# The first projections of a one-core attention and mixture-of-experts step: raw tokens transposed, the norm factor put in at the copies, the first weight block in four pieces, zero products while TensorE waits

## Chip, cores and metric

One core of one Trainium2 chip runs the whole step. The metric is the device time of one execution in microseconds (us). A change of less than 0.2% cannot be told from none by a measurement of this kernel.

## What is computed

The reference is one layer over 256 prompt tokens and 8 × 4 new tokens of a sampled batch, all in float32:

```python
def rmsnorm(x, g):
    xf = x.astype(jnp.float32)
    y = xf * lax.rsqrt(jnp.mean(xf * xf, axis=-1, keepdims=True) + RMS_EPS)
    return (y * g.astype(jnp.float32)).astype(x.dtype)

def project_inputs(x, norm_g, w_in, pos):
    h = rmsnorm(x, norm_g)
    qa, ka, va, qb, kb, vb, qc, gate_logits = jnp.split(h @ w_in, np.cumsum(IN_SPLITS)[:-1].tolist(), axis=-1)
    ...
```

Behind it come three attentions (a window of 128, three dilations, 256 memory tokens, for the sampled batch over caches of 2048 positions), sigmoid gates from `gate_logits` on the merged branches, `w_out`, a second norm, and a mixture of 32 experts of which each token takes 4, with a last norm. The factor 1/sqrt(mean square) is one number for each token (a row of x) and the gain `g` one for each column, so `h @ w_in` is also that factor times `((x * g) @ w_in)`.

## The kernel before

The program is written by hand for each engine, and semaphores hold the engines together; nothing plans the order. The 288 tokens are three tiles t of 128, 128 and 32 (`NTOK`). The model width of 1024 is 8 chunks k of 128.

The start goes like this. SyncE issues the loads in the order of its code: the two prompt tiles (L446, L447), the sampled tokens (L448), the identity matrix (L449), `params` with the gains (L450), weight block 0 (L460), the rest of the constants (L535), weight block 1 (L460). ScalarE takes the sum of squares of each tile as it lands (L699) and its root (L707). VectorE makes the factor of the norm from it (`inverse_roots`, L1657 to L1661). Then the rows of x are multiplied by their factor into `h_tok`: tiles 0 and 2 by VectorE (`scale_rows`, L1665), tile 1 by ScalarE (L718). TensorE transposes h in six groups of four chunks (`transposes`, L1001, against the identity matrix), and VectorE copies each group from PSUM (`ps`) to `hT`, which lies in `arena`, and multiplies it by the gain (`evict_tr`, L1678). Only then come the projections:

```python
for n in range(5):
    wblk_ready(pe, n)
    pe.wait_ge(S["tr_evicted"], 6)
    for t in range(3):
        for k in range(KC): ...
```

There are five blocks n of columns (four of 512, one of 256). A block is two tiles of 8 products of 128x512 (L1034) and the 32 sampled tokens, whose 8 chunks go to four row groups of PSUM and are added by VectorE (L1707 to L1710). The weights have two buffers (`wblk`, in `ring`), and block n + 2 is issued by SyncE when the products of block n are done (`wait_wblk_used`), with a copy of a piece of a cache in HBM behind it (L483). ScalarE copies the projections to `q_tok` and `kv` (L735 to L747), with the fixed factor `QSCALE` for the queries.

In the third block the transposes of the memory tokens (their own norm; L718, L1001) are put in. After the fifth block TensorE waits for the weights of the memory projection (L1043), and after these it transposes the queries and keys (L1001) between the products of the gates (L1065), which read `hT` again, all 288 tokens as the moving operand. VectorE turns the queries and keys before that (`rope`, L1727 to L1732). GpSimd loads the memory tokens when block 0 has landed (L651).

Much later, SyncE starts a stream of 192 pieces of 2 MB of expert weights through eight buffers (L578): each piece is issued when TensorE has used what lay in its buffer before.

## Time and profile before

| what | value |
|---|---|
| three runs | 1329.03, 1330.87 and 1331.73 us, median 1330.87 us |
| the profiled execution | 1324.62 us, its span 1322.8 us |
| TensorE busy in the span | 1275.8 us, 96% |
| VectorE, ScalarE, GpSimd busy | 340.8, 213.0 and 27.5 us |
| mean granted TensorE clock | 0.992 |
| moved by DMA | 498.76 MB |

### The profile page before, as it was taken

What the parts mean: (1) busy time and instruction counts of PE and PEld (TensorE: products, weight loads), DVE (VectorE), ACT (ScalarE), POOL (GpSimd) and SP (SyncE); (2) the same over time, 40 slices, a digit from 0 to 9 for tenths busy, and PEclk for the clock granted to TensorE, in tenths of its full rate; (3) what the DMA queues carried; (4) which work ended last, traced back from release to release, by engine and by line L of the source; (5) the groups of instructions that cost most, each with busy time, mean ns of one, the idle gap of its engine ahead of it and who ended that gap; (6) DMA issues with size and microseconds to landing.
All of it is one profiled execution on the core that took longest, in us unless ns stands there. A gap on an engine that the chain in (4) does not pass through costs nothing.

```text
span 1322.8 us, 14782 instructions
## 1 busy us (share of the span) xinstructions
PE 1275.8 (96%) x6332; PEld 526.7 (40%) x6332; DVE 340.8 (26%) x735; ACT 213.0 (16%) x442; POOL 27.5 (2%) x42
## 2 busy tenths in 40 slices
PE   6999997999999999999999999999999999999996
PEld 3446666667543333333333333333333333333332
DVE  2243552323533221211222122121211212121213
ACT  2212433223111011011110101111011101101012
POOL 0000004200000000000000000000000000000000
PEclk9999998999999999999999999999999999999998
DMA  6675998789779999999999999999999999999994
GB/s 252 253 270 231 355 367 276 227 265 352 294 279 397 402 427 427 428 428 428 427 427 428 427 427 429 429 428 427 429 427 427 428 428 427 428 428 427 428 426 173
DMA packets 71013, 498.76 MB, mean 377 GB/s; under 512 B 5808, under 2 KB 28976, under 8 KB 45584
## 3 DMA queue, kind: packets, MB, share of 16 engines
q1 hardware_dynamic: 70032, 495.15, 92.1%
q0 software_dynamic: 912, 2.62, 0.5%
q8 instruction: 52, 0.85, 0.3%
q14 instruction: 17, 0.14, 0.0%
HBM read 495.29 MB, written 36.96 MB: 402 GB/s over the span
## 4 chain that ended last, share of the span: by engine, by line
PE 81%; DMA 14%; DVE 2%; ACT 1%; issue 0%; SPq 0%; DVEq 0%
PE ps L1540 27%; PE ps L1577 15%; DMA ring<-in_w_gate_up 13%; PE ps L1065 7%; PE ps L1464 6%; PE ps L1509 5%; PE ps L1034 5%; PE ps L1354 2%; PE ps L1346 2%; PE ps L1228 2%; PE ps L1212 1%; PE ps L1475 1%; PE ps L1557 1%; PE ps L1043 1%; PE ps L1517 1%; PE ps L1294 1%
## 5 line engine op out<-in xcount | busy, mean ns | idle before, releaser
L1540 PE MATMUL ps<-ring,cring 128*64 128x512 f32 x1552 | 352.9, 598 | 5.8 <-DMA ring<-in_w_gate_up 5.8
L1540 PEld LDWEIGHTS ps<-ring,cring 128*64 128x64 f32 x1552 | 106.0, 137 | 226.0 <-issue 204.4
L1577 PE MATMUL ps<-ring,cring 128*64 128x512 f32 x752 | 171.5, 598 | 0.7 <-issue 0.7
L1930 DVE TENSOR_TENSOR cring<-ps,params 128x512 f32<-128x512 f32 x32 | 22.1, 691 | 424.2 <-PE ps L1475 424.2
L2028 DVE TENSOR_TENSOR x_tok<-x_tok,ps 128x1024 f32<-128x1024 f32 (+1 forms) x51 | 53.0, 1040 | 225.3 <-PE ps L1509 225.3
L1065 PE MATMUL ps<-arena,ring 128*128 128x288 f32 x384 | 102.3, 412 | 2.1 <-ACT ring L771 2.1
L926 ACT ACTIVATE cring<-ps 128x512 f32<-128x512 f32 x32 | 19.1, 597 | 488.6 <-PE ps L1557 488.6
L1464 PE MATMUL ps<-h_tok,cring 128*64 128x512 f32 x372 | 91.1, 607 | 0.0
L1577 PEld LDWEIGHTS ps<-ring,cring 128*64 128x64 f32 x752 | 50.1, 136 | 102.4 <-issue 99.7
L1065 PEld LDWEIGHTS ps<-arena,ring 128*128 128x128 f32 x384 | 69.6, 189 | 25.6 <-issue 4.6
L1034 PE MATMUL ps<-ring,arena 128*128 128x512 f32 (+3 forms) x240 | 73.1, 561 | 0.5 <-DVE arena L1678 0.5
L1540 PE MATMUL ps<-late,cring 128*64 128x512 f32 x256 | 59.5, 596 | 1.6 <-DMA late<-in_w_gate_up 0.8
L1540 PE MATMUL ps<-arena,cring 128*64 128x512 f32 x240 | 55.8, 595 | 0.0
L936 ACT ACTIVATE cring<-ps 64x512 f32<-64x512 f32 x32 | 18.9, 590 | 226.1 <-PE ps L1577 226.1
L1509 PE MATMUL ps<-cring 128*128 128x512 f32 (+1 forms) x96 | 52.6, 630 | 0.7 <-issue 0.7
L1509 PE MATMUL ps<-pT,cring 128*128 128x512 f32 (+1 forms) x96 | 49.3, 596 | 0.0
L1034 PEld LDWEIGHTS ps<-ring,arena 128*128 128x128 f32 (+1 forms) x240 | 32.7, 165 | 39.8 <-issue 38.9
L1943 DVE TENSOR_TENSOR cring<-cring 128x512 f32<-128x512 f32 x32 | 22.2, 693 | 85.7 <-ACT cring L922 85.6
L1464 PEld LDWEIGHTS ps<-h_tok,cring 128*64 128x64 f32 x372 | 21.1, 134 | 47.1 <-issue 43.4
L1354 PE MATMUL ps<-ring,arena 128*128 128x512 f32 (+1 forms) x96 | 33.4, 599 | 0.0
L918 ACT ACTIVATE cring<-ps 128x512 f32<-128x512 f32 x32 | 19.1, 597 | 86.0 <-PE ps L1464 82.5
L1577 PE MATMUL ps<-arena,cring 128*64 128x512 f32 x144 | 32.8, 597 | 0.0
(325 smaller groups left out, 1001.8 us busy)
## 6 DMA issues: line engine op xcount, KB each, us to landing
ring<-in_w_gate_up SPq DMA_DIRECT2D x97, 2048.0 KB, 24.7
ring<-in_w_down SPq DMA_DIRECT2D x47, 2048.0 KB, 27.1
late<-in_w_gate_up SPq DMA_DIRECT2D x16, 2048.0 KB, 24.3
arena<-in_w_gate_up SPq DMA_DIRECT2D x15, 2048.0 KB, 26.3
ring<-in_w_in SPq DMA_DIRECT2D x10, 2048.0 KB, 11.0
late<-in_w_down SPq DMA_DIRECT2D x8, 2048.0 KB, 26.4
arena<-in_w_down SPq DMA_DIRECT2D x8, 2048.0 KB, 25.8
out_dil_k_s<-in_cache_dil_k SPq DMA_DIRECT2D x8, 2044.0 KB
```

Of the source, the lines that this page charges most:

```text
L1034: ins = pe.matmul(bank((n % 2) * 3 + t)[k_rows(t, k), 0:b - a], hT_v[:, k, TOK0[t]:TOK0[t] + NTOK[t]], wblk[n % 2][:, k, 0:b - a], **k_gro ...
L1065: ins = pe.matmul(bank(gate_bank(m))[:, 0:TT], wblk[(6 + m // 4) % 2][:, k, (m % 4) * P:(m % 4 + 1) * P], hT_v[:, k, :], start=(k == 0), s ...
L1228: return pe.matmul(out, lhs, rhs, start=start, stop=last, skip_group_check=True)
L1346: ins = pe.matmul(bank(3 * (dt % 2) + br)[:, 0:TT], wblk[blk % 2][:, k, (dt % 4) * P:(dt % 4 + 1) * P], oT[:, k, :], start=(k == ks[0]), s ...
L1354: ins = pe.matmul(bank(wout_bank[t][n])[k_rows(t, k), :], hT_v[:, k, TOK0[t]:TOK0[t] + NTOK[t]], wo[n][:, k, :], **k_group(t, k))
L1464: ins = pe.matmul(bank(6)[64 * h:64 * h + 64, :], sel[0:n, t, :], h_v[0:n, t, h * 512:(h + 1) * 512], start=(t == 0), stop=(t == 2), skip_ ...
L1509: ins = pe.matmul(out, gateT[:, tok] if first else selT[:, tok], b_dn[:, 512 * h:512 * h + 512] if first else y2[h], start=True, stop=True ...
L1540: ins = pe.matmul(bank(gu0 + u)[64 * h:64 * h + 64, :], xTe[:, k % 4, (k // 4) * 64:(k // 4) * 64 + 64], pair_buf[slot][:, a:a + 512], sta ...
L1577: ins = pe.matmul(bank(7 if last else 5)[64 * h:64 * h + 64, :], aT[:, kk % 4, (kk // 4) * 64:(kk // 4) * 64 + 64], pair_buf[slot][:, a:a ...
L1930: v.tensor_tensor(xTe4, xps, gain_x, ALU.mult).then_inc(S["xt_ready"], 1)
L1943: v.tensor_tensor(act, u_clip, g_sig, ALU.mult).then_inc(S["act_ready"], 1)
L2028: v.tensor_tensor(xs, xs, rows, ALU.add).then_inc(S["sc_added"], 1)
```

## The change

- The six first transposes take `x_tok` and not `h_tok`, so they wait for the load of x alone. `hT` then holds x times the gain, and the factor of the norm is put in where ScalarE copies the projections (`q_scale`, which is the factor times `QSCALE`, and `norm_st[16..18]`). VectorE makes all three factors at once, after the six copies, and `scale_rows` of VectorE and the ScalarE one for tile 1 are gone.
- The gates read `hT` too. So, after block 4, TensorE multiplies a matrix of ones with a diagonal of the factors (three small products into bank 6), and VectorE multiplies the whole `hT` by the result (128x2304, one instruction between its turns of tile 0 and tile 1). The first transposes of the queries wait for it.
- Weight block 0 is loaded in four pieces of two chunks, and the loads of x tile 1 and of the sampled tokens are issued between them. TensorE's code for block 0 is written out by hand: two products of tile 0 as each piece lands, a group of transposes between them.
- VectorE clears 384 columns of `pT` first, and TensorE multiplies zeros (`warm_up`, 256 columns each, into bank 5, which nobody reads): four before the first transposes, three behind the second group.

```diff
@@ -285,6 +285,9 @@
         norm_st = stat[:, 180:204]
+        q_scale = norm_st[:, 21:24]
+        rstd_diag = pT[:, 0:TT]
+        warm = pT[:, 512:896]
         s_st = stat[:, 204:256]
@@ -294,7 +297,7 @@
             for c in (0, 4):
-                tr_groups.append(([h_v[0:NTOK[t], t, (c + j) * P:(c + j + 1) * P] for j in range(4)],
+                tr_groups.append(([x_v[0:NTOK[t], t, (c + j) * P:(c + j + 1) * P] for j in range(4)],
                                   hT_v[:, c:c + 4, TOK0[t]:TOK0[t] + NTOK[t]], gain_v[:, 0, c:c + 4]))
@@ -444,8 +447,6 @@
             sp.dma_start(x_v[:, 0, :], d["x_prompt"][0, 0:P, :]).then_inc(S["x0_in"], 16)
-            sp.dma_start(x_v[:, 1, :], d["x_prompt"][0, P:SEQ, :]).then_inc(S["x1_in"], 16)
-            sp.dma_start(x_v[0:NS, 2, :], d["x_sample"].rearrange("b i n -> (b i) n")).then_inc(S["x2_in"], 16)
             sp.dma_start(ident, d["consts"][:, 0:P]).then_inc(S["id_in"], 16)
@@ -531,7 +532,16 @@
                 assert 16 * outs == KV_OUT
-            load_wblk(0)
+            def load_first(k, s):
+                a, b = qkv_cols[0]
+                sp.dma_start(wblk[0][:, k:k + 2, :], w_in[:, k:k + 2, a:b]).then_inc(S[s], 16)
+
+            load_first(0, "w0a_in")
+            sp.dma_start(x_v[:, 1, :], d["x_prompt"][0, P:SEQ, :]).then_inc(S["x1_in"], 16)
+            load_first(2, "w0b_in")
+            sp.dma_start(x_v[0:NS, 2, :], d["x_sample"].rearrange("b i n -> (b i) n")).then_inc(S["x2_in"], 16)
+            load_first(4, "w0c_in")
+            load_first(6, "wblk0_in")
             sp.dma_start(cst[:, P:], d["consts"][:, P:]).then_inc(S["cst_in"], 16)
@@ -718,8 +728,6 @@
             act_e.wait_ge(S["rstd"], 1)
-            scale_rows(x_v[:, 1, :], h_v[:, 1, :], P, 1)
-
             for n in range(5):
@@ -730,21 +738,22 @@
                     q, kvt = q_tok[0:r, t, :], kv[0:r, t, :]
+                    qs, ks = q_scale[0:r, t:t + 1], norm_st[0:r, 16 + t:17 + t]
                     if n == 0:
...
                         ins = act_e.activation(q[:, 0:512].rearrange("p (j v n) -> p v j n", v=2, n=HD),
-                                               pb.rearrange("p (v j n) -> p v j n", v=2, n=HD), ACT.Copy, scale=QSCALE)
+                                               pb.rearrange("p (v j n) -> p v j n", v=2, n=HD), ACT.Copy, scale=qs)
                     elif n == 1:
-                        act_e.activation(kvt[:, 0:128], pb[:, 0:128], ACT.Copy)
-                        act_e.activation(kvt[:, 384:512], pb[:, 128:256], ACT.Copy)
-                        ins = act_e.activation(q[:, 512:768], pb[:, 256:512], ACT.Copy, scale=QSCALE)
+                        act_e.activation(kvt[:, 0:128], pb[:, 0:128], ACT.Copy, scale=ks)
+                        act_e.activation(kvt[:, 384:512], pb[:, 128:256], ACT.Copy, scale=ks)
+                        ins = act_e.activation(q[:, 512:768], pb[:, 256:512], ACT.Copy, scale=qs)
                     elif n == 2:
-                        ins = act_e.activation(q[:, 768:1280], pb, ACT.Copy, scale=QSCALE)
+                        ins = act_e.activation(q[:, 768:1280], pb, ACT.Copy, scale=qs)
                     elif n == 3:
-                        act_e.activation(kvt[:, 128:384], pb[:, 0:256], ACT.Copy)
-                        ins = act_e.activation(kvt[:, 512:768], pb[:, 256:512], ACT.Copy)
+                        act_e.activation(kvt[:, 128:384], pb[:, 0:256], ACT.Copy, scale=ks)
+                        ins = act_e.activation(kvt[:, 512:768], pb[:, 256:512], ACT.Copy, scale=ks)
                     else:
-                        ins = act_e.activation(q[:, 1280:1536], pb[:, 0:256], ACT.Copy, scale=QSCALE)
+                        ins = act_e.activation(q[:, 1280:1536], pb[:, 0:256], ACT.Copy, scale=qs)
                     ins.then_inc(S["proj_evicted"], 1)
@@ -1011,32 +1020,68 @@
+            def proj_products(n, t, ks):
+                a, b = qkv_cols[n]
+                for k in ks:
+                    ins = pe.matmul(bank((n % 2) * 3 + t)[k_rows(t, k), 0:b - a],
+                                    hT_v[:, k, TOK0[t]:TOK0[t] + NTOK[t]], wblk[n % 2][:, k, 0:b - a],
+                                    **k_group(t, k))
+                if ks[-1] == KC - 1:
+                    ins.then_inc(S["proj_done"], 1)
+
+            def warm_up(n):
+                for _ in range(n):
+                    pe.matmul(bank(5)[:, 0:256], warm[:, 0:P], warm[:, P:3 * P], start=True, stop=True)
+
+            pe.wait_ge(S["warm_ready"], 1)
+            warm_up(4)
             pe.wait_ge(S["id_in"], 16)
-            for g in range(6):
-                pe.wait_ge(*((S["hn_v"], 1), (S["hn_done"], 1), (S["hn_v"], 2))[g // 2])
-                if g >= 2:
-                    pe.wait_ge(S["tr_evicted"], g - 1)
-                transposes(g)
-
-            for n in range(5):
+            pe.wait_ge(S["x0_in"], 16)
+            transposes(0)
+            transposes(1)
+            warm_up(3)
+            pe.wait_ge(S["tr_evicted"], 1)
+            pe.wait_ge(S["w0a_in"], 16)
+            proj_products(0, 0, range(0, 2))
+            pe.wait_ge(S["x1_in"], 16)
+            transposes(2)
+            pe.wait_ge(S["w0b_in"], 16)
+            proj_products(0, 0, range(2, 4))
+            pe.wait_ge(S["tr_evicted"], 2)
+            transposes(3)
+            pe.wait_ge(S["w0c_in"], 16)
+            proj_products(0, 0, range(4, 6))
+            pe.wait_ge(S["x2_in"], 16)
+            pe.wait_ge(S["tr_evicted"], 3)
+            transposes(4)
+            wblk_ready(pe, 0)
+            proj_products(0, 0, range(6, 8))
+            pe.wait_ge(S["tr_evicted"], 4)
+            transposes(5)
+            proj_products(0, 1, range(KC))
+            pe.wait_ge(S["tr_evicted"], 6)
+            proj_products(0, 2, range(KC))
+
+            for n in range(1, 5):
                 wblk_ready(pe, n)
-                pe.wait_ge(S["tr_evicted"], 6)
-                a, b = qkv_cols[n]
                 for t in range(3):
...
                         for g in range(6, TR_H):
-                            pe.wait_ge(S["hn_done"], g // 2 - 1)
+                            pe.wait_ge(S["hn_done"], g // 2 - 2)
                             pe.wait_ge(S["tr_evicted"], g - 1)
...
                         pe.wait_ge(S["proj_evicted"], 3 * (n - 2) + t + 1)
-                    for k in range(KC):
-                        ins = pe.matmul(bank((n % 2) * 3 + t)[k_rows(t, k), 0:b - a],
-                                        hT_v[:, k, TOK0[t]:TOK0[t] + NTOK[t]], wblk[n % 2][:, k, 0:b - a],
-                                        **k_group(t, k))
-                    ins.then_inc(S["proj_done"], 1)
+                    proj_products(n, t, range(KC))
+            pe.wait_ge(S["cst_in"], 16)
+            pe.wait_ge(S["diag_ready"], 1)
+            pe.wait_ge(S["tr_evicted"], TR_H)
+            for t in range(3):
+                tok = slice(TOK0[t], TOK0[t] + NTOK[t])
+                ins = pe.matmul(bank(6)[:, tok], const("ones")[0:NTOK[t], :], rstd_diag[0:NTOK[t], tok],
+                                start=True, stop=True)
+            ins.then_inc(S["rstd_rows"], 1)
             wblk_ready(pe, W_MEM)
-            pe.wait_ge(S["tr_evicted"], TR_H)
             for t in range(2):
@@ -1078,6 +1123,7 @@
             wblk_ready(pe, 6)
+            pe.wait_ge(S["hT_scaled"], 1)
             pe.wait_ge(S["proj_evicted"], 15)
@@ -1660,11 +1706,7 @@
-            def scale_rows(t):
-                r = NTOK[t]
-                v.tensor_scalar(h_v[0:r, t, :], x_v[0:r, t, :], norm_st[0:r, 16 + t:17 + t], None, ALU.mult) \
-                    .then_inc(S["hn_v"], 1)
-
+            v.memset(warm, 0.0).then_inc(S["warm_ready"], 1)
             link(v.memset(norm_st, 1.0))
@@ -1678,16 +1720,16 @@
-            link(inverse_roots(0, 1, 1))
-            scale_rows(0)
-            signal(inverse_roots(1, 2, 2), "rstd")
             v.wait_ge(S["params_in"], 16)
-            evict_tr(0, 0)
-            evict_tr(1, 1)
-            link(inverse_roots(2, 3, 3))
-            scale_rows(2)
-            for g in range(2, 6):
+            for g in range(6):
                 evict_tr(g, g)
+            link(inverse_roots(0, 3, 3))
+            v.tensor_scalar(q_scale, norm_st[:, 16:19], QSCALE, None, ALU.mult).then_inc(S["rstd"], 1)
+            for t in range(3):
+                r = NTOK[t]
+                ins = v.tensor_scalar(rstd_diag[0:r, TOK0[t]:TOK0[t] + r], ident[0:r, 0:r], norm_st[0:r, 16 + t:17 + t], None,
+                                      ALU.mult)
+            ins.then_inc(S["diag_ready"], 1)
@@ -1714,6 +1756,10 @@
             for t in range(3):
+                if t == 1:
+                    v.wait_ge(S["rstd_rows"], 1)
+                    v.tensor_tensor(hT_v, hT_v, bank(6)[:, 0:TT].unsqueeze(1).to_broadcast([P, KC, TT]), ALU.mult) \
+                        .then_inc(S["hT_scaled"], 1)
                 v.wait_ge(S["proj_evicted"], 12 + t + 1)
```

TensorE's queue from the start of the program, in the kernel before (`x_tok` and `h_tok` are x and its scaled form, `arena` here the identity matrix or `hT`, `ring` the weight block, and [waits ...] names the semaphores that a row waits for):

```order
L1001 MATMUL ps<-arena,h_tok 128x128 [waits hn_v,id_in]
L1001 MATMUL ps<-arena,h_tok 128x128 x3
L1001 MATMUL ps<-arena,h_tok 128x128 [waits hn_v]
L1001 MATMUL ps<-arena,h_tok 128x128 x3
L1001 MATMUL ps<-arena,h_tok 128x128 [waits tr_evicted,hn_done]
```

TensorE's queue at the same place in the changed kernel, to the end of block 0's first tile:

```order
L1034 MATMUL ps<-pT 128x256 [waits warm_ready]
L1010 MATMUL ps<-arena,x_tok 128x128 [waits x0_in,id_in]
L1034 MATMUL ps<-pT 128x256 x3
L1026 MATMUL ps<-ring,arena 128x512 [waits w0a_in,tr_evicted]
L1010 MATMUL ps<-arena,x_tok 128x128 [waits x1_in]
L1026 MATMUL ps<-ring,arena 128x512 [waits w0b_in]
L1010 MATMUL ps<-arena,x_tok 128x128 [waits tr_evicted]
L1026 MATMUL ps<-ring,arena 128x512 [waits w0c_in]
L1010 MATMUL ps<-arena,x_tok 128x32 [waits tr_evicted,x2_in]
L1026 MATMUL ps<-ring,arena 128x512 [waits wblk0_in]
L1010 MATMUL ps<-arena,x_tok 128x32 [waits tr_evicted]
```

Each row with a wait stands for the first of its group; the rest of a group follows without one. The waits for the norm (`hn_v`, `hn_done`) are gone, and six products of tile 0 stand ahead of the last two groups of transposes.

SyncE's queue, in the kernel before:

```order
L446 DMA x_tok<-in_x_prompt 128x1024
L447 DMA x_tok<-in_x_prompt 128x1024
L448 DMA x_tok<-in_x_sample 32x1024
L449 DMA arena<-in_consts 128x128
L450 DMA params<-in_params 128x330
L460 DMA ring<-in_w_in 128x8x512
L535 DMA arena<-in_consts 128x3253
L460 DMA ring<-in_w_in 128x8x512
```

And in the changed kernel:

```order
L449 DMA x_tok<-in_x_prompt 128x1024
L450 DMA arena<-in_consts 128x128
L451 DMA params<-in_params 128x330
L537 DMA ring<-in_w_in 128x2x512
L540 DMA x_tok<-in_x_prompt 128x1024
L537 DMA ring<-in_w_in 128x2x512
L542 DMA x_tok<-in_x_sample 32x1024
L537 DMA ring<-in_w_in 128x2x512 x2
L545 DMA arena<-in_consts 128x3253
L461 DMA ring<-in_w_in 128x8x512
```

The identity matrix moved up to second place; the bytes ahead of the end of block 0, and ahead of the end of block 1, are the same. There are three issues more.

## Rows read from the trace of the kernel before

**Rows 1.** The page: the chain that ended last, shares of the span.

```profile
PE 81%; DMA 14%; DVE 2%; ACT 1%; issue 0%; SPq 0%; DVEq 0%
```

**Rows 2.** Timeline 0 to 15 us: start, duration, instruction [idle before <-releaser].

```profile
0.80 0.08 DVE L1668 MEMSET stat<- 128x24 f32 x1 [0.80 <-PEq L2141]
...
8.00 1.94 PE L1001 MATMUL ps<-arena,h_tok 128*128 128x128 f32 x8 [8.00 <-DVE h_tok L1665]
...
13.04 0.41 PE L1001 MATMUL ps<-arena,h_tok 32*128 32x32 f32 x4 [0.84 <-DVE arena L1678]
...
14.51 31.02 PE L1034 MATMUL ps<-ring,arena 128*128 128x512 f32 x79 [0.48 <-DVE arena L1678]
```

**Rows 3.** Timeline of block 0: two weight loads at half clock; tiles 0, 1; block 1.

```profile
17.34 0.33 PEld L1034 LDWEIGHTS ps<-ring,arena 128*128 128x128 f32 x1 [0.52 <-issue]
18.19 0.33 PEld L1034 LDWEIGHTS ps<-ring,arena 128*128 128x128 f32 x1 [0.52 <-issue]
...
23.35 0.60 ACT L735 ACTIVATE cring<-ps 128x512 f32<-128x512 f32 x1 [12.95 <-PE ps L1034]
...
30.22 0.60 ACT L735 ACTIVATE cring<-ps 128x512 f32<-128x512 f32 x1 [6.27 <-PE ps L1034]
...
31.96 0.30 PEld L1034 LDWEIGHTS ps<-ring,arena 128*128 128x128 f32 x2 [0.84 <-issue]
```

**Rows 4.** Busy time by stretch: PE, PEld, DVE, ACT, POOL, PEclk, DMA share, GB/s.

```profile
13.00:14.00 1.00, 0.77 (x8) 0.64 (x8) 0.77 (x2) 0.00 (x0) 0.67 (x1) 1.00 1.08 455
...
14.50:15.25 0.75, 0.74 (x2) 0.47 (x3) 0.00 (x0) 0.00 (x0) 0.00 (x0) 1.00 0.78 330
15.25:18.65 3.40, 3.40 (x5) 1.33 (x4) 0.96 (x1) 0.00 (x0) 0.00 (x0) 0.50 0.99 384
18.65:20.00 1.35, 1.35 (x4) 0.57 (x3) 0.00 (x0) 0.00 (x0) 0.00 (x0) 1.00 1.05 408
```

**Rows 5.** DMA issues of 0 to 26 us: KB each, median us to landing.

```profile
arena<-in_consts SPq DMA_DIRECT2D x1, 64.0 KB, 5.2
params<-in_params SPq DMA_DIRECT2D x1, 165.0 KB, 5.0
```

**Rows 6.** Landings: both weight blocks of L460, then the three loads of x.

```profile
DMA to landing us min/median/max: 9.9/15.3/20.7
...
DMA to landing us min/median/max: 3.8/5.3/5.4
```

**Rows 7.** Timeline: SyncE's issues of x tile 0, params, weight blocks 0 and 1.

```profile
0.72 0.41 SPq L446 DMA_DIRECT2D x_tok<-in_x_prompt  x1
...
2.59 0.49 SPq L450 DMA_DIRECT2D params<-in_params  x1
3.12 0.43 SPq L460 DMA_DIRECT2D ring<-in_w_in  x1
...
4.22 0.44 SPq L460 DMA_DIRECT2D ring<-in_w_in  x1
```

**Rows 8.** Timeline 60 to 106 us: transposes at full clock, VectorE's turns, the memory block.

```profile
61.59 1.04 PE L1001 MATMUL ps<-arena,ring 128*128 128x128 f32 x8
...
91.82 14.00 PE L1043 MATMUL ps<-ring 128*128 128x512 f32 x32 [1.71 <-DMA ring<-in_w_mem_kv]
...
94.41 0.20 DVE L1732 TENSOR_TENSOR late<-late 128x48 f32<-128x48 f32 x1
...
99.62 0.19 DVE L1732 TENSOR_TENSOR late<-late 32x48 f32<-32x48 f32 x1
...
105.66 1.04 PE L1001 MATMUL ps<-arena,cring 128*128 128x128 f32 x8
```

**Rows 9.** The page's groups: VectorE with a PSUM operand, 128x1024.

```profile
L2028 DVE TENSOR_TENSOR x_tok<-x_tok,ps 128x1024 f32<-128x1024 f32 (+1 forms) x51 | 53.0, 1040 | 225.3 <-PE ps L1509 225.3
```

**Rows 10.** Waits: who <- whom: us in total, times, longest; SyncE's queue first.

```profile
SPq L578 <- PE ps L1540: 507.4, 124, 10.6
...
PE ps L1540 <- DMA ring<-in_w_gate_up: 5.8, 6, 1.2
```

More of the change, by code:

```diff
@@ L226, in build @@
         names = """x0_in x1_in x2_in mem_in id_in cst_in params_in tail_self wblk0_in wblk1_in kc0_in kc1_in
-        out_dma copy_dma v_self zeros sumsq root rstd ssum_ready hn_v hn_done tr_done tr_evicted proj_done
-        proj_evicted rope_done gate_done gate_evicted gates_ready
+        out_dma copy_dma v_self zeros sumsq root rstd ssum_ready hn_done tr_done tr_evicted proj_done
+        proj_evicted w0a_in w0b_in w0c_in diag_ready rstd_rows hT_scaled warm_ready rope_done gate_done gate_evicted gates_ready
         scores_done stat_ready exp_done p_ready pt_done pt_evicted pv_done o_evicted
@@ L1438, in _ @@
             pe.wait_ge(S["sel0_ready"], 1)
-            pe.wait_ge(S["hn_done"], 4)
+            pe.wait_ge(S["hn_done"], 3)
             pe.wait_ge(S["rt_evicted"], 3)
             gather_rows(2)
-            pe.wait_ge(S["hn_done"], 5)
+            pe.wait_ge(S["hn_done"], 4)
             gather_rows(0)
@@ L1450, in _ @@
             ins.then_inc(S["cnt_done"], 1)
-            pe.wait_ge(S["hn_done"], 6)
+            pe.wait_ge(S["hn_done"], 5)
             pe.wait_ge(S["sel_ready"], 1)
@@ L1639, in _ @@
             chain = [0]
-            told = {}
+            told = {"rstd": 1}
             def signal(ins, name):
```

## The prediction

> **What bounds the kernel now.** I read the chain of waits first. It is TensorE for 81% and DMA for 14% [rows 1], so a microsecond taken out of TensorE's way early should reach the end, unless a transfer with its own time stands in between. Next comes the timeline of the start, where TensorE has nothing to do: its first instruction is at 8.00, put down to VectorE's scaled rows, and its first product of the projections at 14.51 [rows 2]. Then it has few gaps. Block 1 starts at 31.96 [rows 3], and this is the point that I follow: behind it the order on TensorE and the loads are as before. The reader is to see two losses ahead of it. TensorE waits for the norm, which is not needed for a transpose; and the first products run on a low clock: 1.00 from 14.50 to 15.25, then 0.50 (1.2 GHz) for 3.4 us, then 1.00 (2.4 GHz) again, after a stretch in which TensorE worked in pieces, 0.77 of the microsecond from 13 [rows 4].
>
> Two more views tell whether a gain lasts. SyncE's queue waits 507.4 us in all for TensorE to free the buffers of the expert stream [rows 10]: the stream is started by TensorE and moves with it. TensorE waits for that stream for only 5.8 us [rows 10].
>
> **Prices.** At 1.2 GHz the weight loads of one pass are 0.85 us apart, and a product has two, so it takes 1.71 us [rows 3]. At 2.4 GHz a tile of eight takes 30.22 - 23.35 = 6.87, 0.86 for each [rows 3]. A zero product has half the columns: 0.86 low, 0.43 high. Eight transposes of 128 take 1.94 [rows 2] or, at the high clock, 1.04 [rows 8]; four of the 32-token tile 0.41 [rows 2]. The sampled tile of block 0 takes 31.96 - 30.11 = 1.85, 30.11 being the end of tile 1, 0.11 before ScalarE's copy [rows 3].
>
> **When the data are there.** Tile 0 of x lands at 0.72 + 3.8 = 4.5 [rows 6, 7]. By 2.59 + 5.0 = 7.6 the `params` are in, and with them 1381 KB [rows 5, 7]. Block 0, 2048 KB more, is in at 3.12 + 9.9 = 13.0: 379 KB for each us. Block 1 lands at 4.22 + 20.7 = 24.9 [rows 6, 7]. The queue is served in order, so in the new order: identity 5.0 (second issue, 1.19 + 3.8; bounds 4.5, and 6.4 with its own 5.2 of [rows 5]); first piece 1253 KB, before 7.6; x tile 1, 1765 KB, 8.6; second piece 2277 KB, 10.0; third 2917 KB, 11.7; fourth, as before, 13.0. The three extra issues of some 0.47 us [rows 7] lie beside the transfers. If they counted in full, block 1 would land at 26.3.
>
> **TensorE, step by step.** VectorE clears 384 columns: between 0.08 (24 columns, [rows 2]) and 0.39 (1.04 us for 1024 columns, [rows 9]); I take the upper, TensorE starts at 1.3. Four zero products at the low clock, 3.4 us, end at 4.7. Transposes of tile 0 from 5.0, 1.94, to 6.95. Three zero products: 1.3 or 2.6, by the clock. No row of before shows TensorE busy so early, so the clock is the unknown. The near row is the one in which it rose after 3.4 us of dense work [rows 4]; here work is dense from 1.3 but for 0.3 us. I take the rise at about 7: products start at 8.25. From there to block 1 the work is tile 0 6.87, two groups of four transposes 1.04, two small groups 0.82, tile 1 6.87, sampled tile 1.85: 17.45 us, all at 2.4 GHz. Each piece is there before its turn, by 0.5 us or more (second piece 10.0, wanted at 10.5; fourth 13.0, wanted at 14.9). Block 1 starts at 25.7, and its weights landed at 24.9. **Gain 31.96 - 25.7 = 6.3 us.**
>
> Seen in another way: before, block 0 took 31.96 - 14.51 = 17.45, of which 15.59 (6.87 + 6.87 + 1.85) is work at the high clock and 1.9 the low stretch. Now it starts at 8.25 and holds 1.86 of transposes that used to stand ahead of it. That is 14.51 - 8.25 - 1.86 = 4.4 from the earlier start and 1.9 from the clock. The scaling and the roots are off VectorE and ScalarE ahead of the transposes; only so can the start move.
>
> **Bounds of this term.** If the clock rises at 5.0, products start at 7.6 and block 1 at 25.0: 6.9, and the landing at 24.9 caps it at 7.0. If it rises only behind the zero products, they end at 9.55 and block 1 starts at 27.0: 5.0. If the products then also have a low stretch like that of before, 3.4 us at half [rows 4], 1.7 more is lost: 3.3.
>
> **What is added later.** The factor of the norm is made by VectorE after the last copy, near 17.3 + 1.5 us. ScalarE's copy of tile 0 waits for that to about 19. Behind it stand only copies, and TensorE needs the bank in block 2; ScalarE idled 6.27 before its second copy [rows 3]. Price nothing; without that cover, at most 2.4 us once. The three products with the ones, at most 0.21 each (a quarter of 0.86), fall into the 1.71 us in which TensorE waits for the memory weights [rows 8]; without that wait they would cost 0.6. The multiply of `hT` has 2304 columns with a PSUM operand: 2304/1024 × 1.04 = 2.3 us [rows 9]. It starts when VectorE has turned tile 0, at 94.6, ends at 96.9, and is wanted at 105.66; behind it the other turns move from 99.8 to 102.1, also before 105.66 [rows 8]. Spare 3.5 us: it would have to take 5.9 us to be seen. Below nothing: no part of this can gain. Price 0, bounds 0 and 0.6.
>
> **The sum.** 1324.62 - 6.3 = 1318.3 for the execution that was profiled. That one stands 6.25 us below the median of the three runs, 1330.87, so the runs should have **1324.6 us**.
>
> **Rivals.**
>
> *The pieces come late.* If the queue does not serve them one by one, or each costs time, TensorE sits in the middle of tile 0. With all four at 13.0, 17.45 us of work follow, block 1 starts at 30.5: gain 1.5, and none if the idle time brings the low stretch back (1.7). For it: nothing smaller than the whole block was ever waited for here. Against: x, `params`, block 0 and block 1 landed at 4.5, 7.6, 13.0 and 24.9, in order of issue [rows 5 to 7]. Time 1329.4 to 1331.1; chance 0.06.
>
> The Trainium skill, "DMA: Bandwidth & Descriptors", section "Rules for kernel authors", speaks for this rival: it wants 1 MiB or more in a DMA for full bandwidth, and its section on the anatomy of a DMA gives each about 2.0 us of fixed time. If three more such costs stood one after another, an estimate by that page, block 1 would land at 30.9 and the gain would be 1.1. The rows disagree: `params`, 165 KB, issued 0.47 us behind the identity, landed at 7.6, by the same rows some 0.3 us behind it [rows 5].
>
> *TensorE stays at 1.2 GHz through block 0.* This is the one that ends slower. The zero products hold the queue to 9.55 at the low clock, and 17.45 us of work become 34.9: block 1 starts at 44.5, 12.5 us later than before, 1343.4 us. It decides from a low stretch of 9.9 us behind the zero products (27.0 + 9.9/2 = 31.96). For it: the clock did fall at 15.25, with TensorE at work [rows 4]. Against: it fell behind work in pieces, and rose after 3.4 us of dense work. Chance 0.03.
>
> The Trainium skill, "TensorE: Matmul & The Clock Gate", section on the clock gate, has seen the clock stuck low for over 50 us; no row here shows that.
>
> *The gain does not reach the end.* A transfer whose time does not depend on TensorE would take it back. Only block 1 is such a one, at 24.9 to 26.3, which leaves 5.7 at the worst. The later loads are issued when TensorE frees a buffer. If something unseen takes all, 1330.9; chance 0.05.
>
> *The clock rises late*, at 9.5 or after: 3.3 to 5.0 gained, 1325.9 to 1327.6; chance 0.18.
>
> **How the numbers follow.** The forecast (5.0 to 7.0 gained) has 0.68. Low end: 1330.87 - 7.0 = 1323.9, less 1.9 for the spread of the runs (the lowest was 1.84 below the median) = 1322.0. High end: 1330.87 - 3.3 = 1327.6, and 1.0 for the spread (the highest was 0.86 above) = 1328.6. Outside lie the late pieces, the gain that is lost, and the slow case, 0.14 together. 0.2% is 2.7 us, about what a measurement of this kernel can tell from no change. Faster: forecast and late clock, and a part of nothing else, 0.86. Same: late pieces, lost gain, 0.10. Slower: 0.04.
>
> **What would show it.** The zero products near 1.3, the transposes near 5.0, put down to the loads and no more to VectorE; the first product near 8.2; the granted clock at 1.00 before 10 and through block 0; block 1 at 25.0 to 27.0; between the products of tile 0 no wait of over 0.5 us; the memory weights waited for as long as before, less the three small products; the multiply of `hT` at 2 to 3 us, waited for by nobody; the span shorter by what block 1 came earlier. The prediction is wrong if block 1 starts after 27.0, if PEclk shows 0.50 behind 10, or if the shift at block 1 is not found again at the end of the span.

## The result: 9.7 us faster on record, 6 to 7 us in the longer series

| | before | after |
|---|---|---|
| median of the recorded runs | 1330.41 us (1329.03 to 1331.73, 4 runs) | 1320.69 us (1316.95 to 1322.89, 4 runs) |
| the profiled execution, its span | 1324.62, 1322.8 us | 1316.95, 1315.1 us |
| TensorE busy | 1275.8 us | 1278.5 us |
| block 1 starts | 31.96 us | 26.60 us |

The fourth run of before is 1329.96 us. The medians differ by 9.7 us; the ratio is 0.9929 with a 95% interval of [0.9902, 0.9957], which is 5.7 to 13.0 us. The direction was forecast; the size was 6.3 us, and the time, 1320.69, lies below the low end of the range, 1322.0. Two longer series below give the same change 6.8 and 6.1 us.

TensorE's queue at the start of the changed kernel, from the timeline:

```profile
1.30 3.45 PE L1034 MATMUL ps<-pT 128*128 128x256 f32 x8 [1.30 <-DVE pT L1709]
4.77 1.09 PE L1010 MATMUL ps<-arena,x_tok 128*128 128x128 f32 x8
5.69 1.46 PE L1034 MATMUL ps<-pT 128*128 128x256 f32 x6
7.61 1.95 PE L1026 MATMUL ps<-ring,arena 128*128 128x512 f32 x4 [0.45 <-DMA ring<-in_w_in]
9.40 0.60 PE L1010 MATMUL ps<-arena,x_tok 128*128 128x128 f32 x4
10.97 1.98 PE L1026 MATMUL ps<-ring,arena 128*128 128x512 f32 x4 [0.97 <-DMA ring<-in_w_in]
12.79 0.60 PE L1010 MATMUL ps<-arena,x_tok 128*128 128x128 f32 x4
13.23 1.88 PE L1026 MATMUL ps<-ring,arena 128*128 128x512 f32 x4
...
17.68 12.62 PE L1026 MATMUL ps<-ring,arena 128*128 128x512 f32 x40
```

VectorE's scaled rows are gone as a releaser [rows 2], and the first product stands at 7.61 in place of 14.51. Two waits for pieces have come in, 0.45 and 0.97. The transposes take 1.09, near the 1.04 of the high clock [rows 8].

Busy time by stretch of the same start (columns as in [rows 4]), then the timeline at the memory weights and the multiply of `hT`:

```profile
0.00:4.70 4.70, 3.40 (x8) 2.51 (x8) 0.47 (x3) 1.64 (x3) 2.14 (x5) 1.00 0.52 162
...
7.60:13.00 5.40, 4.42 (x14) 2.17 (x15) 0.69 (x1) 2.89 (x6) 0.00 (x0) 1.00 1.05 350
```

```profile
84.67 1.04 PE L1081 MATMUL ps<-pT,arena 128*128 128x128 f32 x6
...
85.99 14.00 PE L1088 MATMUL ps<-ring 128*128 128x512 f32 x32 [0.27 <-DMA ring<-in_w_mem_kv]
...
89.28 2.56 DVE L1761 TENSOR_TENSOR arena<-arena,ps 128x2304 f32<-128x2304 f32 x1
```

The 1.71 us of waiting [rows 8] became 0.27 behind the three products with the ones: they fill a wait, and save nothing. The multiply takes 2.56 us, and nobody waits for it in the list of waits.

The page's chain, the chief waits of TensorE (who <- whom: total, times, longest), and two of SyncE's queue:

```profile
PE 82%; DMA 14%; DVE 2%; ACT 1%; SPq 0%; issue 0%; DVEq 0%
```

```profile
PE ps L1586 <- DMA ring<-in_w_gate_up: 6.7, 6, 2.3
PE ps L1258 <- DMA cring<-in_cache_mem_k: 4.2, 1, 4.2
...
SPq L588 <- PE ps L1586: 507.3, 124, 10.6
```

The bound and the expert stream are as before [rows 1, 10]. The second row is a wait that the prediction did not look at: TensorE stands for the third keys of the cached positions, 5.9 us in the profile of before. So the two profiled spans differ by 7.7 us: 5.4 at block 1 (31.96 - 26.60), 0.5 more by the memory weights (91.82 - 85.99 = 5.8), 1.7 at that later wait, and the 0.1 or so that is left behind it.

### The profile page after: what moved, and what is told of

Same layout as the page of the kernel before. It is cut to its first block, busy times and chain, and to the rows that moved or that the text cites. A ratio compares the mean times of both kernels' runs of the same rounds, so it can differ in the third digit from the quotient of the medians.

```text
span 1315.1 us, 14816 instructions
## 1 busy us (share of the span) xinstructions
PE 1278.5 (97%) x6352; PEld 528.9 (40%) x6352; DVE 341.3 (26%) x729; ACT 214.1 (16%) x441; POOL 27.5 (2%) x42
## 4 chain that ended last, share of the span: by engine, by line
PE 82%; DMA 14%; DVE 2%; ACT 1%; SPq 0%; issue 0%; DVEq 0%
PE ps L1586 27%; PE ps L1623 15%; DMA ring<-in_w_gate_up 13%; PE ps L1110 7%; PE ps L1510 6%; PE ps L1555 5%; PE ps L1026 5%; PE ps L1400 2%; PE ps L1392 2%; PE ps L1274 2%; PE ps L1258 1%; PE ps L1521 1%; PE ps L1603 1%; PE ps L1088 1%; PE ps L1563 1%; PE ps L1340 1%
## 6 DMA issues: line engine op xcount, KB each, us to landing
arena<-in_w_gate_up SPq DMA_DIRECT2D x15, 2048.0 KB, 26.2
```

## The experiments

The theory: block 1 starts earlier by as much as TensorE's start allows, and the end moves by the same. Rivals: the end moves by more, because the early start helps a later wait; or the gain comes from one part of the change alone (zero products, raw transposes) and not from the pieces. Ratios are to the kernel before in the same series, with 95% intervals.

### Both kernels again

*Before, again:*

> The kernel before, unchanged, a second time. Theory A (the change brings block 1 forward by 5.4 us, the rest of the gain is what the later DMA waits and low clock stretches happen to cost in a run): ratio 1.000, the runs 1325 to 1332 us, and the wait for the third key cache near 223 us differs from the 5.9 us of the first trace by 1 us or more. Theory B (the later waits belong to the kernel): the wait is 5.9 us again within 0.3.

Measured: 1.0001 [0.9982, 1.0021], a median of 1328.65 us. The wait for the third keys was 7.4 us, as theory A allows and B does not. Block 1 started at 33.20: its first products ran low for longer than in the first profile.

*Changed, again:*

> The changed kernel, unchanged, a second time. Theory A: block 1 at 26.6 us again, the wait for the third key cache anywhere from 4 to 6.5 us, gain in the runs 5.5 to 8 us. Theory B: the wait is 4.2 us again within 0.3, and the gain is 8 to 10 us.

Measured: 1321.26 us, 0.9949 [0.9931, 0.9967], 6.8 us faster. Block 1 started at 27.38, not at 26.6 again. The wait was 4.0 us, as B says; the gain is that of A.

*Changed, a third time:*

> The changed kernel as it is, a second time, with its own profile. Theory (the start gives 5.4 to 5.8 us, all of which reaches the end, and the rest of the difference seen on record is where the clock happened to fall): ratio 0.994 to 0.996 (5.5 to 7.5 us), block 1 starts at 26.6 to 27.2, third keys waited for between 4 and 7.5 us, as in the kernels that start later. Rival (the earlier start also shortens the wait for the third keys by some 2 us, as a rule): that wait is 3.5 to 4.5 again, and the ratio 0.993 or less.

Measured: 1322.40 us, 0.9954 [0.9934, 0.9974], 6.1 us faster. Block 1 started at 27.60, later than the theory's 27.2. The wait for the third keys was 4.0 us in both repeats, which spoke for the rival; the ratio did not.

*Before, a third time:*

> The kernel before again, to see its wait for the third keys a third time (so far 5.9 and 7.4 us, against 4.2, 4.0 and 4.0 in three profiles of the changed kernel). If the earlier start shortens this wait as a rule, it is 5.5 to 7.5 us here. If it is chance, from the pace of the queue, it may as well be 4 us. Ratio 1.000 either way, between 0.998 and 1.002.

Measured: 1.0001 [0.9980, 1.0021]. The wait is shorter than in any profile of the changed kernel:

```profile
PE ps L1212 <- DMA cring<-in_cache_mem_k: 3.7, 1, 3.7
```

The wait was 5.9, 7.4 and 3.7 us before, and 4.2, 4.0 and 4.0 after. Two versions below settle more of it. The one without zero products starts block 1 at 26.75, as early as the changed kernel, and waits 6.2 us; the one with the delay waits 6.3. So the wait does not go with the start of block 1: a late start had the shortest and an early one a long one. What is left is that it differs between executions. A small systematic part is not excluded.

### The same start, with the gain given back in front of block 1

```diff
             transposes(5)
             proj_products(0, 1, range(KC))
+            warm_up(12)
             pe.wait_ge(S["tr_evicted"], 6)
             proj_products(0, 2, range(KC))
```

> The changed kernel with twelve more zero products (0.43 us each at 2.4 GHz, 5.15 us in all) between tiles 1 and 2 of block 0, so that its early work is all there but block 1 starts at 31.8 to 33, as in the kernel before. Theory A (only the time at which block 1 starts counts; the wait for the third key cache is a full DMA queue whose pace differs from run to run): runs within 1.5 us of the kernel before plus or minus its noise, ratio 0.998 to 1.001, and that wait anywhere from 4 to 7.5 us. Rival (the changed start shortens the wait for the third key cache by something else than the shift): a wait near 4.1 us and 1.5 to 3 us faster than the kernel before.

Measured: 0.9998 [0.9985, 1.0011]. The twelve products took 5.34 us at the high clock, and block 1 started at 32.13. The wait for the third keys was 6.3 us, where the rival wanted 4.1. The whole gain is gone: nothing else in the change, early loads, fewer instructions on VectorE and ScalarE, is worth anything that can be seen (the interval is 1.7 us to either side).

### Without the zero products

```diff
-            warm_up(4)
             pe.wait_ge(S["id_in"], 16)
...
-            warm_up(3)
```

> The changed kernel without its seven zero products. Theory A (the clock costs only where TensorE is not waiting for a piece of block 0 anyway): transposes of tile 0 from 5.0 at 1.2 GHz, first product near 7.6 for the first piece, the second piece still waited for or just met at 11.0, the clock up by 12, block 1 at 26.6 to 28.5, so 0 to 2 us of the gain lost. Rival (the zero products carry the gain): the clock stays low into tile 1, block 1 at 29 or later, 2.5 us or more lost.

Measured: 1322.66 us, 0.9964 [0.9945, 0.9983]. Its timeline:

```profile
4.68 1.94 PE L1010 MATMUL ps<-arena,x_tok 128*128 128x128 f32 x8 [4.68 <-DMA arena<-in_consts]
7.53 3.43 PE L1026 MATMUL ps<-ring,arena 128*128 128x512 f32 x4 [0.91 <-DVE arena L1718]
10.79 0.60 PE L1010 MATMUL ps<-arena,x_tok 128*128 128x128 f32 x4
11.23 1.88 PE L1026 MATMUL ps<-ring,arena 128*128 128x512 f32 x4
```

The transposes and the first two products run at 1.2 GHz, 3.43 us in place of 1.95, and yet block 1 starts at 26.75, against 26.60 to 27.60 in three profiles of the changed kernel. The slow products lie where TensorE would wait for the second piece. In this version the zero products buy nothing that the profiles show at block 1. By the medians of the one series this kernel is 1.4 us slower (1322.66 for 1321.26), and the intervals overlap: neither nothing nor some 3 us is excluded.

### Without the pieces

```diff
-            load_first(0, "w0a_in")
...
-            load_first(2, "w0b_in")
...
-            load_first(4, "w0c_in")
-            load_first(6, "wblk0_in")
+            load_wblk(0)
```

TensorE does all transposes first, then the products of block 0.

> The changed kernel with block 0 in one load behind both other loads of x, all transposes ahead of its products. Theory A (what the pieces bring is the work that fits ahead of the landing of block 0, near 13.3): products from 13.3, 15.6 us of them at 2.4 GHz, block 1 at 29.0; if TensorE's idle time from about 10 lets the clock fall once, 1.7 more, 30.7. So 2.4 to 4.1 us of the gain lost. Rival (pieces slow the loading down by as much as they bring): block 1 within 1 us of 26.6.

Measured: 1326.57 us, 0.9994 [0.9975, 1.0013]: no gain. Its timeline and its busy time by stretch:

```profile
13.59 2.93 PE L1023 MATMUL ps<-ring,arena 128*128 128x512 f32 x3 [3.22 <-DMA ring<-in_w_in]
```

```profile
8.00:11.00 3.00, 1.82 (x16) 1.39 (x16) 2.08 (x6) 2.65 (x6) 0.00 (x0) 1.00 1.04 384
11.00:15.00 4.00, 1.41 (x2) 0.84 (x3) 1.30 (x8) 0.00 (x0) 0.88 (x1) 0.66 1.08 433
15.00:19.00 4.00, 4.00 (x6) 1.48 (x5) 0.96 (x1) 0.00 (x0) 0.00 (x0) 0.50 0.98 382
```

TensorE finishes the transposes early, stands for 3.22 us, and the clock that it had gained is lost in that wait, between 12 and 13. Block 1 starts at 32.09, where the expectation had 30.7 at the latest: the low stretch lasts to about 19.2, and block 0 took 18.50 us where 15.59 is the work at the high clock, so it cost 2.9 and not 1.7; the products also began 0.3 later. All of the gain is lost, not 2.4 to 4.1 us of it. Without the pieces the rest of the change is worth nothing that can be seen, though the raw transposes alone, below, are worth some. What the pieces bring with the scaled rows of before was not run.

### Raw transposes alone

The kernel before with its own order of loads and whole block 0, no zero products; the transposes read `x_tok`, and the norm factor goes in at the copies and in `hT` as in the changed kernel. Of its edit against before, the wait of the transposes:

```diff
-                pe.wait_ge(*((S["hn_v"], 1), (S["hn_done"], 1), (S["hn_v"], 2))[g // 2])
+                pe.wait_ge(S[f"x{g // 2}_in"], 16)
```

> Raw tokens transposed and the norm put in later, but the loads in the old order and whole, no zero products, block 0's products behind all transposes. Theory A (without pieces, block 0's landing near 13.3 is the wall): transposes from 7.4, products from 13.4 to 13.6 instead of 14.5, block 1 at 29.3 to 31.5 by the clock, so 1 to 2.5 us better than the kernel before, and 4 us or more of the gain missing. Rival (taking the norm off the way is what gains): 4 us or more better.

Measured: 1324.23 us, 0.9984 [0.9968, 0.9999], 2.1 us. The transposes start only at 7.30, behind the identity matrix, which here is still the fourth load. The products start at 13.28, where block 0 has just landed, and block 1 at 30.96.

### Zero products alone

```diff
+            pe.wait_ge(S["warm_ready"], 1)
+            warm_up(10)
             pe.wait_ge(S["id_in"], 16)
             for g in range(6):
...
                 transposes(g)
+                if g in (1, 3):
+                    warm_up(2)
```

VectorE clears the zeros first, as in the changed kernel.

> The kernel before with ten zero products ahead of its first transposes and two behind each of the first two tiles' groups. Theory A (the clock is worth what its low stretch costs in block 0, 1.9 us in one trace and 3.1 in the other, and transposes at the high clock save little as they wait for the norm): block 1 at 29.8 to 31.3, 1.5 to 3 us faster. Rival (TensorE falls back to 1.2 GHz while it waits for the norm and the block): block 1 at 32 or later, nothing gained.

Measured: 1324.60 us, 0.9978 [0.9959, 0.9998], 2.9 us. In the stretch in which before shows 0.50 [rows 4]:

```profile
14.01:19.00 4.99, 4.99 (x12) 2.36 (x13) 0.96 (x1) 0.00 (x0) 0.16 (x1) 1.00 0.97 384
```

The low stretch is gone and block 1 starts at 29.76. Both this gain and that of the raw transposes are at the edge of what the times can tell (their intervals reach to 0.2 and 0.1 us); the profiles show them at block 1. So the zero products are worth something where the products stand behind a start in pieces of work, and not where TensorE waits for data anyway.

### The later wait: three cache copies issued behind the cache loads

The changed kernel; the copies from cache to cache in HBM are delayed (none is left out):

```diff
-                copy_cache()
+                if i == 9:
+                    copy_cache()
...
-            while copies:
+            while len(copies) > 1:
...
+            copy_cache()
+            copy_window("k")
+            copy_window("v")
```

> The changed kernel with three of the copies from cache to output in HBM (one of 2 MB, both window copies) issued behind piece 4 of the expert stream, where the DMA engines idle from 350 to 360 us, instead of ahead of the third key cache. Theory A (the wait of 4.2 us for that cache is the copies' backlog, and the clock falls in it): the wait is under 1 us, no low stretch near 220 us, 4 to 6 us faster than the changed kernel (ratio to the kernel before 0.990 to 0.992), if the pieces of the stream still come in time. Rival (the wait is the latency of the load itself): still 3 us or more. Third: the copies only move the loss into the expert stream, which then waits 4 us more for its pieces at the end.

Measured: 1317.09 us (6 runs), 0.9923 [0.9902, 0.9944], 10.2 us. The 5 us ahead of the first issue for the third keys and the 3.4 us behind the wait, in the changed kernel; then the wait and the same 5 us in this one:

```profile
201.29:206.29 5.00, 3.35 (x37) 2.75 (x33) 1.39 (x2) 2.55 (x6) 2.95 (x6) 1.00 1.18 435
...
215.90:219.30 3.40, 3.40 (x17) 3.40 (x18) 1.32 (x2) 0.60 (x1) 2.96 (x7) 0.50 0.83 252
```

```profile
PE ps L1263 <- DMA cring<-in_cache_mem_k: 2.0, 2, 1.0
```

```profile
202.76:207.76 5.00, 3.35 (x37) 2.76 (x33) 1.38 (x2) 2.55 (x6) 3.46 (x7) 1.00 0.33 97
```

The load finds a DMA share of 0.33 in place of 1.18. From its first issue to the end of the wait it is 6.4 us (207.76 to 214.15) in place of 9.6 (206.29 to 215.84). Two waits of 1.0 us stand in place of one of 4.2, more than the 1 us in all that was expected; the ratio lies just above the expected 0.990 to 0.992. And the clock, which in the changed kernel was at 0.50 for 3.4 us behind the wait, is at 1.00 from 200 to 230: an estimate from these rows is 2.2 us of waiting and 1.7 of clock, 3.9 together, where the ratios, of different series, give 3.4 to 4.1. The expert stream did not pay for it: it was waited for 5.3 us, against 6.7.

*The same deferral in the kernel before:*

> The kernel before with the deferral alone (three of the cache copies are issued behind the cache loads, so that the third keys find a shorter queue). Theory (the wait for the third keys is a full DMA queue and has nothing to do with the start, so both gains add): wait of 2 us or less in place of 5.8 to 7.4, 3 to 5 us faster than the kernel before, ratio 0.9963 to 0.9980, and the deferred kernel with the change's start is then 5.4 to 6.3 us below it. Rival (the queue's stall takes up an earlier start, so the two are tied together): this one is as fast as the deferred kernel with the change's start, about 0.992 to 0.993; or the deferral brings nothing here, 1.000.

Measured: 1324.31 us, 0.9971 [0.9954, 0.9989], 3.8 us, the wait 1.7 in two parts. By point estimates the start adds 0.9971 - 0.9923 = 0.0048 or 6.4 us on top of it, as much as without the deferral. So the two gains add as far as these series tell; the two ratios are of different series, and their intervals leave some 3.6 us to either side. That the stall took up the whole early start is excluded.

*The deferral, and the second piece ahead of tile 1 of x:*

```diff
             load_first(0, "w0a_in")
-            sp.dma_start(x_v[:, 1, :], d["x_prompt"][0, P:SEQ, :]).then_inc(S["x1_in"], 16)
             load_first(2, "w0b_in")
+            sp.dma_start(x_v[:, 1, :], d["x_prompt"][0, P:SEQ, :]).then_inc(S["x1_in"], 16)
```

TensorE takes the products of pieces 1 and 2 ahead of tile 1's transposes.

> The changed kernel with the same deferral, and the second piece of block 0 issued ahead of tile 1 of x, TensorE's code turned to match (products of pieces 1 and 2, then the transposes of tile 1). Theory (TensorE stood 1.4 us for pieces because x tile 1 lay in the queue ahead of piece 2): the wait of 0.97 us in the middle of tile 0 is gone, block 1 starts 0.5 to 1.0 us earlier, at 25.7 to 26.2, and the time is 0.5 to 1 us below the deferred kernel: ratio 0.991 to 0.993. Rival (the total of bytes decides): a wait of the same length comes at piece 3 or at x tile 1, block 1 starts at 26.6 as in the changed kernel, and the ratio is that of the deferred kernel, 0.992 to 0.993.

Measured: 1317.85 us (6 runs), 0.9922 [0.9894, 0.9950]. One wait of 0.50 us is left, for the third piece:

```profile
8.02 3.60 PE L1031 MATMUL ps<-ring,arena 128*128 128x512 f32 x8
11.45 1.04 PE L1015 MATMUL ps<-arena,x_tok 128*128 128x128 f32 x8
12.99 1.98 PE L1031 MATMUL ps<-ring,arena 128*128 128x512 f32 x4 [0.50 <-DMA ring<-in_w_in]
```

Block 1 starts at 26.46, 1.2 us earlier than in the deferred kernel's profile (27.66), but not at the expected 25.7 to 26.2, and within 0.2 us of the earliest profile of the changed kernel. The result lies between the theory and the rival: the wait has moved to the third piece and is half as long. The time does not tell the two apart. Both beat the changed kernel by point estimate, by 0.0026 to 0.0032 in ratio, some 4 us, in other series than its own; their intervals overlap in part with its own.

### What the parts show together

Start of block 1 in each profile, and the gain from the series' ratio:

| kernel | block 1 earlier than before's mean, 32.31 | gain measured, us |
|---|---|---|
| changed (three profiles, mean 27.19) | 5.1 | 6.8 and 6.1 |
| without zero products | 5.6 | 4.8 |
| without pieces | 0.2 | 0.8 |
| with the delay | 0.2 | 0.3 |
| raw transposes alone | 1.4 | 2.1 |
| zero products alone | 2.6 | 2.9 |

Before's mean is that of 31.96, 33.20 and 31.78; the changed kernel's that of 26.60, 27.38 and 27.60. Every gain follows from the start of block 1 to within 2 us, which is about the half width of one interval.

## Why the prediction was right, and where it was wrong

**What bounds the kernel: right.** Time taken out of TensorE's way at the start reached the end, and the delay took all of it back. The chain of waits missed one, though: the 5.9 us for the third keys, whose length differs from run to run.

**The zero products and the clock: early.** VectorE's clearing, start at 1.3 and four zero products in 3.4 us were as forecast (3.45). The rise was taken at about 7; the transposes at 4.77 already cost 1.09. In the six other profiles that begin with the same zero products they took 1.04, 1.04, 1.31, 1.47, 1.60 and 1.92: the moment varies, and that it came early on record was in part luck. The first product came at 7.61, the bound that the prediction gave for an early rise, and there the first piece held it. The near row of the prediction, a low stretch of 3.4 us, varies too: in the repeat of before with block 1 at 33.20 the weight loads were 0.85 us apart from 15.52 to 19.79.

**"Each piece is there before its turn, by 0.5 us or more": this step failed.** The pieces were estimated at under 7.6, 10.0, 11.7 and 13.0. The second was waited for until 10.97, and the fourth released GpSimd at 14.21, against 13.33 before. From 7.6 to 13.0 the DMA engines moved 350 GB/s; the same stretch of before:

```profile
7.60:13.00 5.40, 3.69 (x16) 3.08 (x16) 4.59 (x16) 2.73 (x6) 0.00 (x0) 1.00 1.10 412
```

In the repeats of the changed kernel it was 357 and 331, in those of before 410 and 402, and with the whole block in the new order 394. So the pieces cost pace, and the new order a little; why smaller loads move slower is not shown. They did not cost 2 us each one after another: block 1, issued at 6.04, landed 19.7 us later at 25.7 against 24.9, 0.8 us later (1.6 and 1.8 in the repeats). The estimate by the Trainium skill, "DMA: Bandwidth & Descriptors", section on the anatomy of one DMA, was 6; the page fits those 2.0 us on DMAs that GpSimd issues, and SyncE issues these. The page's advice of 1 MiB or more for full bandwidth, section "Rules for kernel authors", agrees with these rows in direction: with four pieces of 512 KB the stretch moved 331 to 357 GB/s, with the whole block in the same order 394, which is 9 to 16% less.

The late second piece is 0.97 us of waiting, and the seams between products and transposes cost 0.57 more (block 0 took 26.60 - 7.61 = 18.99 for a forecast 17.45). With the earlier first product (0.64) block 1 stood at 26.60 for a forecast of 25.7, and the gain was 5.4 for 6.3. The same sum holds in the repeats: first piece at 8.16 and 8.22, second piece waited for 1.20 and 1.36 us, the same 17.45 and 0.57, block 1 at 27.38 and 27.60. These lie beyond 27.0, which the prediction had named as a sign of being wrong; by the mean of three profiles the gain at block 1 is 5.1, at the low end of its bounds. Block 1 landed 0.8 to 0.9 us ahead of its own first product in all three, so little is left to be gained by starting block 0 earlier still.

**What is added later: right.** The three products with the ones took 1.04 us together, above the bound of 0.6, but fell into the wait all the same. The multiply of `hT` took 2.56 for 2.3, with no one waiting. ScalarE's first copy came at 19.19 for a forecast 19.

**The sum: the base and the spread failed, and this put the time out of the range.** The prediction subtracted 6.3 from a median of three runs, 1330.87, and took 1.9 us as their spread. The 128 runs of before in the series here have their median at 1326.9 and reach from 1322.48 to 1334.11; a third are at 1329 or above. The three shown were all of that third, and so was the fourth. Of the changed kernel 28 runs, with the four on record, have a median of 1321.6, from 1316.95 to 1325.35. The medians differ by 5.3 us and the means by 6.3, where block 1 came 5.1 earlier in the means of the profiles. The long median less the forecast gain would have been 1326.9 - 6.3 = 1320.6, against 1321.6 measured, and the forecast gain itself fits both longer series. So the mis-sized term is the base. For the profiled execution the sum gave 1318.3, and 1316.95 was measured; then 6.25 was put on top as the distance from the profile to the runs, and by the 128 runs this is 1326.9 - 1324.62 = 2.3. That is 4.0 us too much. Of the 9.7 us on record some 4 belong to which runs were compared, 3.5 of before (1330.41 for 1326.9) and 0.9 of the changed kernel (1320.69 for 1321.6).

Much of what makes that spread is seen in the profiles. TensorE's clock in one stretch, around the router, in before, in its third profile and in the changed kernel:

```profile
372.00:418.00 46.00, 42.45 (x206) 16.14 (x205) 19.07 (x75) 8.53 (x13) 2.07 (x4) 0.96 0.88 345
```

```profile
372.00:418.00 46.00, 42.92 (x189) 15.48 (x189) 17.98 (x68) 8.53 (x13) 2.07 (x4) 0.81 0.80 310
```

```profile
372.00:418.00 46.00, 43.62 (x193) 14.43 (x191) 17.47 (x62) 5.70 (x8) 1.56 (x3) 0.96 0.93 374
```

From the third keys to the end the first takes 1322.8 - 223.4 = 1099.4 us, the second 1325.2 - 220.8 = 1104.4, the changed kernel 1315.1 - 215.8 = 1099.3. The two with the clock at 0.96 agree to 0.1 us, and the one at 0.81 is 5 us longer. All eleven profiles without the deferral fall in the same two groups: four with the clock at 0.96 to 1.00 in this stretch take 1099.2 to 1100.2 us, seven with 0.81 to 0.89 take 1102.4 to 1105.6. That, and 3.7 to 7.4 us at the third keys, is most of before's range. What decides in an execution whether the clock falls there was not tried, and three profiles of each kernel are too few to say that the change has no part in it.

**The rivals.** Late pieces: half right as a mechanism, 1.4 us of waits on record and 1.8 and 2.3 in the repeats, and not 4.8. TensorE at 1.2 GHz through block 0: in no profile of the six kernels that begin with zero products. The gain lost: no. The clock late: it was early.

## What to carry to other kernels

Start the products on part of the weights, and count what else waits for data before paying for a warmer clock: here the changed start gained nothing without the pieces, and zero products in front of them mostly covered time that was idle anyway. Check every removed wait against the landing of the next load (block 0 at 13, then block 1 at 26). And take the base of a forecast and its range from the places in the profile whose length varies, a full DMA queue or a clock that may fall, and not from three runs.

## What the runs showed of the hardware

The clock column says 1.00 from 0 to 4.70, where four zero products of 256 columns take 3.45 us, 0.86 each. The twelve of the delay take 0.44 each. So the early 1.00 is no granted 2.4 GHz; the column seems to read as full speed until the clock's first record. Durations of like instructions are the better witness: a repeat of before also shows 1.00 at 14.5 to 19.8 with weight loads 0.85 us apart, the spacing of 1.2 GHz [rows 3].

In the version without pieces the clock fell from 1.00 to 0.50 within the wait of 3.22 us, behind some 9 us of zero products and transposes. In the changed kernel it was at 0.50 behind the wait of 4.2 us for the third keys, and with two waits of 1.0 us in its place it stayed at 1.00. The Trainium skill, "TensorE: Matmul & The Clock Gate", section on what is really happening, says that the point at which one kernel gets its clock varies from run to run. The transposes of 1.04 to 1.92 us at the same place of seven profiles agree.
